# Loading each expert weight piece as two half transfers, each with a semaphore of its own, in a one-core hybrid diffusion step

## The chip, the cores and the metric

The kernel runs on one core of a Trainium2 chip. The metric is device time in microseconds (us) of one execution; lower is better. The time before is 1954.64 us, the median of three runs.

## The reference

One inference step of a hybrid backbone layer, on 384 tokens (128 context tokens, 256 latent tokens) of width 1024, in float32. A layer is a mixer (differential attention plus a two-way state space scan) and then a feed-forward part in which each of 16 experts chooses its tokens. The change touches the second part only:

```python
def expert_choice_ffn(h, w_router, w_gate, w_up, w_down):
    cap = EC_FACTOR * ntok // N_EXPERTS
    aff = jax.nn.softmax((xf @ w_router).astype(jnp.float32), axis=-1)
    gates, idx = lax.top_k(aff.T, cap)
    xe = xf[idx]
    he = jax.nn.silu(jnp.einsum('ecd,edf->ecf', xe, w_gate)) * jnp.einsum('ecd,edf->ecf', xe, w_up)
    ye = jnp.einsum('ecf,efd->ecd', he, w_down) * gates[..., None].astype(xe.dtype)
    out = jnp.zeros_like(xf).at[idx.reshape(-1)].add(ye.reshape(-1, d).astype(xf.dtype))
```

An expert sees 16 context and 32 latent tokens. Its three weight matrices hold 3 x 1024 x 2048 floats, 24 MB; all 16 experts hold 402.7 MB, and every byte is read from HBM once.

## The kernel before

**Mixer, routing, gather.** The first half of the program computes the mixer and the routing. Its weights come in 40 transfers of 2 MB (line 797) into two slots. Then the tokens of all experts are gathered.

**Pieces.** The expert weights lie in HBM as `in_expert_chunks[e, c]`, 16 experts of 12 pieces, 192 in all. A piece is 128 rows (one per partition) of 4096 floats, so 16 KB a row and 2,097,152 bytes a piece. Pieces 0 to 7 of an expert are alternate blocks of the gate and the up matrix, pieces 8 to 11 are blocks of the down matrix. SBUF (the program's name for its memory there is `arena`) has six slots of one piece each, and piece c goes to slot (c + 2) mod 6.

**TensorE (PE).** The loop of lines 731 to 786 runs over four groups of four experts. For each piece it waits once, at line 750, for `ff_slot{s}`, the semaphore that the piece's transfer raises by 16, and then issues 16 matmuls at line 765: eight steps k over 128 rows of the contraction, and in each two matmuls q that write the two halves of a PSUM bank. Step k reads floats 512k to 512k + 511 of each row of the slot. The last matmul of a piece raises one of three kinds of semaphore (`ff_used`, `gu_ready`, `d_ready0` or `d_ready1`). Between pieces stand small transposes of the hidden values (line 742). After four experts the outputs are combined (lines 784 and 786), and the next group starts.

**SyncE (SP).** SP issues all expert transfers, in order, at line 800 (`load`). The first six are issued while the mixer still ends. From piece 6 on, `wait_used` (lines 802 to 809) first waits for the semaphore by which PE tells that the piece six before, which lies in the same slot, has been used. The loop over experts is written with `sp.Fori`.

**Others.** ScalarE (ACT) and VectorE (DVE) work on the hidden values between the pieces; at line 1680 DVE writes the gathered tokens of one expert to `xe`.

Of the kernel before, what the change touches and what calls it, by code (L numbers as in the profile page):

```python
# [27 lines left out]
KT = D // P  # L28
EPS = 1e-6
CW = 512  # L30
# [13 lines left out]
FF_SLOTS = 6  # L44
# [20 lines left out]
EC = 12  # L65
# [67 lines left out]
def build(nc, t_in, t_out, consts, scratch):  # L133
    ctx = ExitStack()
    with ctx:
# [4 lines left out]
        def sem(name):  # L140
            if name not in sems:
                sems[name] = ctx.enter_context(nc.semaphore(name))
            return sems[name]
# [14 lines left out]
        slots = [at(16 * s, KT, CW) for s in range(FF_SLOTS)]  # L158
# [102 lines left out]
        mixer_w, expert_w, dt_cols = t_in["mixer_chunks"], t_in["expert_chunks"], t_in["dt_columns"]  # L261
# [21 lines left out]
        def _(pe):  # L283
# [128 lines left out]
            for ts in ((0,), (1, 2)):  # L412
                b = p_bank()
                for i, t in enumerate(ts):
                    for k in range(KT):
                        mm = pe.matmul(b[:, i * 64:(i + 1) * 64], h1T[:, k, t * P:(t + 1) * P], dt_w[:, k, :],
                                       start=k == 0, stop=k == KT - 1)
# [18 lines left out]
            for t in range(NT):  # L436
                pe.matmul(b[:, t * 64:t * 64 + 32], tri_f, tmp_a[:, t, 0:32], start=True, stop=True)
                mm = pe.matmul(b[:, t * 64 + 32:t * 64 + 64], tri_b, tmp_a[:, t, 32:64], start=True, stop=True)
            x_done(mm)
            b = x_bank()  # L440
            mm = pe.matmul(b[:, 0:NT * 64], ones, tmp_a[:, :, :], start=True, stop=True)
            x_done(mm)
            for d, tri in ((0, tri_f), (1, tri_b)):
                b = x_bank()
                for t in range(NT):
                    mm = pe.matmul(b[0:32, t * P:(t + 1) * P], tmp_a[:, t, 32 * d:32 * d + 32], tri,
                                   start=True, stop=True)
# [31 lines left out]
            for u, (g, t) in enumerate(units):  # L479
                if t == 0:  # L480
# [3 lines left out]
                    for d in range(2):  # L484
# [4 lines left out]
                mm = pe.matmul(b[:, 0:P], BC[:, g, TOK[t]:TOK[t] + P], BC[:, 4 + g, TOK[t]:TOK[t] + P],  # L489
                               start=True, stop=True)  # L490
# [3 lines left out]
                if t == 0:  # L494
                    for d in range(2):
# [3 lines left out]
                        for c in range(4):  # L499
                            mm = pe.matmul(b[:, c * P:(c + 1) * P], xdec[:, d, c * P:(c + 1) * P],  # L500
                                           BTM[:, 0, g * P:(g + 1) * P], start=True, stop=True)
                        x_done(mm)
                        AT.setdefault("st", []).append(n_x[0])
                if t == 1:
                    for d in range(2):
                        pe.wait_ge(sem("xdec_ready"), 4 * g + 2 + d + 1)
                        b = x_bank()
                        mm = pe.matmul(b[:, :], BTM[:, 1 + d, g * P:(g + 1) * P], xdec[:, d, :],
                                       start=True, stop=True)
# [10 lines left out]
                for h in range(S_HPG):  # L520
                    o = b[:, h * S_HD:(h + 1) * S_HD]
                    xh = xTM[:, t, h * S_HD:(h + 1) * S_HD]
                    mm = pe.matmul(o, ebuf[:, (2 * u) % 4, h, :], xh, start=True, stop=True)  # L523
                x_done(mm)
                if t:
                    if t == 1:
                        pe.wait_ge(sem("x_free"), hT1_at)
                    for d in range(2):
                        fresh = (t == 1) == (d == 0)
                        b = x_bank()  # L530
                        mm = pe.matmul(b[:, :], BC[:, 4 + g, TOK[t]:TOK[t] + P],  # L531
                                       h0T[:, d, :] if fresh else hT1[:, d, :], start=True, stop=True)
# [6 lines left out]
            for j in range(2):  # L539
                n0 = n_p[0]  # L540
                p_bank(4)
                for k2 in range(2):
                    w = chunk()
                    for ct in range(4):
                        for k in range(KT):
                            mm = pe.matmul(psum[:, (n0 + ct) % 4, 0:NTOK], w[:, k, ct * P:(ct + 1) * P],  # L546
                                           oT[:, k2 * KT + k, :], start=k2 == 0 and k == 0,
                                           stop=k2 == 1 and k == KT - 1)
# [64 lines left out]
            for i in range(NA + 5):  # L613
# [18 lines left out]
                if 3 <= i <= NA + 2:  # L632
# [4 lines left out]
                    for c, vb in kb:  # L637
                        mm = pe.matmul(b[:, 0:P], aT[:, (i - 3) % 2, c * P:(c + 1) * P],
                                       vT[:, vb, h * P:(h + 1) * P], start=c == 0, stop=c == len(kb) - 1)
# [61 lines left out]
            for n in range(4):  # L701
                pe.wait_ge(sem("diag2_ready"), 4 * (n + 1))
                b = p_bank()
                for q in range(4):
                    mm = pe.matmul(b[:, q * P:(q + 1) * P], ones, diag[:, n % 2, q, :], start=True, stop=True)
# [25 lines left out]
            with pe.Fori(0, NE // GE) as g:  # L731
                for i in range(GE):
                    pe.wait_ge(sem("xe_ready"), g * GE + (i + 1))

                    def h_to_cm(j):

                        pe.wait_ge(sem("h_done"), g * 16 + (4 * i + j + 3))
                        pe.wait_ge(sem("hT_done"), g * 16 + (4 * i + j + 1))
                        if i == 0 and j == 0:
                            pe.wait_ge(sem("comb_done"), g * 6 + 2)  # L740
                        for a in range(2):
                            mm = pe.transpose(psum[:, 4, a * P:(a + 1) * P], h_sb[:, j % 2, a * P:(a + 1) * P], ident)  # L742
                        mm.then_inc(sem("hT_psum"), 1)

                    for c in range(12):
                        s = (c + 2) % FF_SLOTS
                        if c == 8:
                            h_to_cm(3)
                            pe.wait_ge(sem("hT_done"), g * 16 + (4 * i + 5))
                        pe.wait_ge(sem(f"ff_slot{s}"), g * 128 + (32 * i + 16 * (c // 6 + 1)))  # L750
                        w = slots[s]
                        if c < 8:
                            j, up = c // 2, c % 2
                            bank, src, k0 = 2 * up + j % 2, xe, 0
                            if not up:
                                pe.wait_ge(sem("h_done"), g * 16 + (4 * i + j + 1))
                        else:
                            j, up = (c - 8) // 2, c % 2
                            bank, src, k0 = 5 + j, hT, KT * up
                            if not up:  # L760
                                pe.wait_ge(sem(f"d_free{j}"), g * GE + (i + 1))
                        first, last = c < 8 or not up, c < 8 or up
                        for k in range(KT):
                            for q in range(2):
                                mm = pe.matmul(psum[HALF * q:HALF * (q + 1), bank, 0:2 * P], src[:, k0 + k, :],  # L765
                                               w[:, k, 2 * P * q:2 * P * (q + 1)], start=bool(first and k == 0),
                                               stop=bool(last and k == KT - 1), tile_position=(0, HALF * q))
                        if c < 8:
                            mm.then_inc(sem("gu_ready" if up else "ff_used"), 1)
                            if up and j:  # L770
                                h_to_cm(j - 1)
                        else:
                            mm.then_inc(sem(f"d_ready{j}" if up else "ff_used"), 1)

                pe.wait_ge(sem("Gcur_ready"), g + 1)
                for j in range(2):
                    pe.wait_ge(sem(f"d_free{j}"), g * GE + (GE + 1))
                pe.wait_ge(sem("hT_done"), g * 16 + 17)
                for n, (t, half) in enumerate([(t, half) for t in range(NT) for half in range(2)]):
                    pe.wait_ge(sem("comb_done"), g * 6 + (n + 1))  # L780
                    bank = (7, 4)[n % 2]
                    cols_ = slice(half * CW, (half + 1) * CW)
                    if t:
                        mm = pe.matmul(psum[:, bank, :], Gs_cur[:, (t - 1) * P:t * P], stage_s[:, cols_], start=True, stop=True)  # L784
                    else:
                        mm = pe.matmul(psum[:, bank, :], Gp_cur, stage_p[:, cols_], start=True, stop=True)  # L786
                    mm.then_inc(sem("comb_ready"), 1)


        @block.sync  # L790
        def _(sp):
            sp.dma_start(cst, consts).then_inc(sem("const_in"), 16)
            for n in range(NM):
                if n >= 2:
                    name, value = AT["chunk_end"][n - 2]
                    sp.wait_ge(sem(name), value)
                sp.dma_start(slots[n % 2].rearrange("p k n -> p (k n)"), mixer_w[n]).then_inc(sem(f"w_in_slot{n % 2}"), 16)
            def load(e, c):
                s = (c + 2) % FF_SLOTS
                sp.dma_start(slots[s].rearrange("p k n -> p (k n)"), expert_w[e, c]).then_inc(sem(f"ff_slot{s}"), 16)  # L800

            def wait_used(e, c):

                if c >= 8 and c % 2:
                    sp.wait_ge(sem(f"d_ready{(c - 8) // 2}"), e + 1)
                elif c % 2:
                    sp.wait_ge(sem("gu_ready"), e * 4 + (c // 2 + 1))
                else:
                    sp.wait_ge(sem("ff_used"), e * 6 + (c // 2 + 1))

            for c in range(12):
                if c == 0:
                    sp.wait_ge(sem("ssd_over"), 1)
                if c == 2:
                    sp.wait_ge(sem("attn_over"), 1)
                if c == 4:
                    sp.wait_ge(sem("p_ready"), AT["chunk_end"][NM - 1][1])
                if c >= 6:
                    wait_used(0, c - 6)
                load(0, c)  # L820
            with sp.Fori(1, NE) as e:
                for c in range(12):
                    wait_used(e - 1 if c < 6 else e, (c - 6) % 12)
                    load(e, c)


        n_store = [0]
# [902 lines left out]
```

## Time and profile before

| | us |
|---|---|
| median of three runs (1953.71, 1954.64, 4177.42) | 1954.64 |
| the profiled execution: its own time | 1952.62 |
| its span, first to last instruction | 1950.8 |
| PE busy in the span, share | 1605.8, 82% |
| DVE busy | 526.8 |
| ACT busy | 256.9 |
| chain that ended last: share of expert transfers (in_expert_chunks) | 31% |
| chain that ended last: share of the expert matmuls (L765) | 14% |

Busy time is the union of an engine's instructions. The chain is followed back from the last instruction, at each step to what released it. The expert part takes the second half of the span, from about 992 us on. One transfer is cut by the hardware into packets, one for each row of the destination, which 16 DMA engines share; the profile tells packets of 4 bytes as well, by which a transfer raises its semaphore, one per engine.

### The profile page before, as it was taken

What the parts mean: (1) busy time and instruction counts of PE and PEld (TensorE: products, weight loads), DVE (VectorE), ACT (ScalarE), POOL (GpSimd) and SP (SyncE); (2) the same over time, 40 slices, a digit from 0 to 9 for tenths busy, and PEclk for the clock granted to TensorE, in tenths of its full rate; (3) what the DMA queues carried; (4) which work ended last, traced back from release to release, by engine and by line L of the source; (5) the groups of instructions that cost most, each with busy time, mean ns of one, the idle gap of its engine ahead of it and who ended that gap; (6) DMA issues with size and microseconds to landing.
All of it is one profiled execution on the core that took longest, in us unless ns stands there. A gap on an engine that the chain in (4) does not pass through costs nothing.

```text
span 1950.8 us, 22828 instructions
## 1 busy us (share of the span) xinstructions
PE 1605.8 (82%) x9379; PEld 950.4 (49%) x9379; DVE 526.8 (27%) x1455; ACT 256.9 (13%) x608; POOL 97.3 (5%) x126
## 2 busy tenths in 40 slices
PE   3997987998999977899698777887769777797775
PEld 1555445555566443454455444544436444364442
DVE  1338778771012034533520001100010000100002
ACT  1232222210010112201200001000010000100001
POOL 1002122120000000000000000000000000000000
PEclk9998999898999988799699999999999999999998
DMA  7124233222233212545259999999999999999993
GB/s 282 76 97 174 87 108 132 106 96 77 86 112 118 105 44 94 213 158 217 87 214 427 428 427 427 426 428 427 427 426 422 426 427 428 422 419 427 427 427 165
DMA packets 40924, 512.94 MB, mean 263 GB/s; under 512 B 4809, under 2 KB 5034, under 8 KB 11130
## 3 DMA queue, kind: packets, MB, share of 16 engines
q1 hardware_dynamic: 33552, 487.15, 60.2%
q0 software_dynamic: 6544, 22.66, 3.5%
q8 instruction: 79, 1.29, 0.3%
q10 hardware_dynamic: 730, 1.68, 0.2%
q14 instruction: 19, 0.16, 0.0%
HBM read 506.65 MB, written 4.82 MB: 262 GB/s over the span
## 4 chain that ended last, share of the span: by engine, by line
PE 52%; DMA 33%; DVE 9%; issue 2%; ACT 1%; POOL 1%; ACTq 0%; SPq 0%; DVEq 0%
DMA arena<-in_expert_chunks 31%; PE psum L333 16%; PE psum L765 14%; PE psum L344 8%; PE psum L546 4%; PE psum L357 1%; PE psum L382 1%; DMA arena<-in_w_subln 1%; PE psum L523 1%; DVE arena L1412 1%; PE psum L784 1%; DVE arena L1489 1%; PE psum L531 1%; DVE arena L1401 1%; PE psum L606 1%
## 5 line engine op out<-in xcount | busy, mean ns | idle before, releaser
L765 PE MATMUL psum<-arena 128*64 128x256 f32 x6144 | 707.5, 386 | 165.9 <-DMA arena<-in_expert_chunks 135.8
L765 PEld LDWEIGHTS psum<-arena 128*64 128x64 f32 x6144 | 433.2, 138 | 430.8 <-DMA arena<-in_expert_chunks 189.5
L333 PE MATMUL psum<-arena 128*128 128x384 f32 x1024 | 355.4, 507 | 10.7 <-ACT arena L1098 7.7
L333 PEld LDWEIGHTS psum<-arena 128*128 128x128 f32 x1024 | 202.3, 199 | 149.3 <-issue 22.3
L1688 DVE TENSOR_TENSOR arena<-arena,psum 128x256 f32<-128x256 f32 x64 | 26.9, 421 | 774.1 <-ACT arena L1153 774.1
L344 PE MATMUL psum<-arena 128*128 128x512 f32 x384 | 166.4, 592 | 1.8 <-DVE arena L1537 1.8
L344 PEld LDWEIGHTS psum<-arena 128*128 128x128 f32 x384 | 72.3, 190 | 90.2 <-issue 87.5
L1153 ACT ACTIVATE arena<-psum 128x256 f32<-128x256 f32 x64 | 24.6, 384 | 612.9 <-PE psum L765 612.9
L382 PE MATMUL psum<-arena 128*128 128x128 f32 (+1 forms) x301 | 57.7, 310 | 54.8 <-DMA arena<-in_g_post_ffn 17.0
L843 POOL TENSOR_TENSOR arena<-arena 128x1 f32<-128x1 f32 x48 | 28.1, 587 | 1224.1 <-DVE arena L1562 941.4
L546 PE MATMUL psum<-arena 128*128 128x384 f32 x256 | 86.0, 500 | 1.8 <-DVE arena L1370 1.2
L1160 ACT ACTIVATE arena<-psum 32x256 f32<-32x256 f32 x128 | 48.0, 375 | 275.2 <-PE psum L765 274.1
L382 PEld LDWEIGHTS psum<-arena 128*128 128x128 f32 (+1 forms) x301 | 39.1, 158 | 81.6 <-issue 45.6
L546 PEld LDWEIGHTS psum<-arena 128*128 128x128 f32 x256 | 49.9, 196 | 37.7 <-issue 2.7
L1412 DVE SCALAR_TENSOR_TENSOR arena<-arena 128x128 f32<-128x128 f32 x192 | 51.4, 344 | 0.0
L357 PE MATMUL psum<-arena 128*32 128x512 f32 x192 | 30.4, 786 | 12.6 <-ACT arena L1098 6.6
L742 PE MATMUL psum<-arena 128*128 128x128 f32 x128 | 27.6, 297 | 15.9 <-DVE arena L1675 15.9
L1098 ACT ACTIVATE arena<-psum,arena 128x384 f32<-128x384 f32 (+1 forms) x48 | 24.0, 505 | 125.0 <-DVE arena L1490 125.0
L523 PE MATMUL psum<-arena 128*128 128x64 f32 x192 | 28.7, 314 | 14.1 <-POOL arena L887 14.1
L606 PE MATMUL psum<-arena 64*128 64x384 f32 (+1 forms) x96 | 20.8, 518 | 23.2 <-ACT arena L1098 22.3
L1696 DVE TENSOR_TENSOR arena<-arena,psum 128x512 f32<-128x512 f32 x24 | 16.5, 687 | 86.0 <-PE psum L786 81.7
L1401 DVE TENSOR_SCALAR arena<-arena 128x128 f32<-128x128 f32 x192 | 38.6, 280 | 0.0
(238 smaller groups left out, 1001.4 us busy)
## 6 DMA issues: line engine op xcount, KB each, us to landing
arena<-in_expert_chunks SPq DMA_DIRECT2D x192, 2048.0 KB, 25.5
arena<-in_mixer_chunks SPq DMA_DIRECT2D x40, 2048.0 KB, 7.9
arena<-cs_rows POOLq DMA_DIRECT2D x24, 512.0 KB, 5.3
arena<-in_state_ssd POOLq DMA_DIRECT2D x8, 256.0 KB, 3.4
out_state<-arena POOLq DMA_DIRECT2D x8, 256.0 KB, 3.4
arena<-in_x_sample ACTq DMA_DIRECT2D x1, 1024.0 KB, 19.5
arena<-in_x_sample POOLq DMA_DIRECT2D x1, 1024.0 KB, 6.7
out_xs<-arena POOLq DMA_DIRECT2D x2, 512.0 KB, 2.9
```

What stands on the lines that cost most here:

```text
L333: mm = pe.matmul(b[:, 0:NTOK], w[:, k, ct * P:(ct + 1) * P], src[:, k, :], start=k == 0, stop=k == KT - 1)
L344: mm = pe.matmul(b[:, :], src[:, k, t * P:(t + 1) * P], w[:, k, :], start=k == 0, stop=k == KT - 1)
L357: mm = pe.matmul(b[32 * q:32 * q + 32, :], cond[:, k, :], w[:, k, :], start=k < 4, stop=k >= 4, tile_position=(0, 32 * q))
L382: mm = pe.transpose(b[0:width, at_:at_ + rows], src, ident[0:rows, 0:rows])
L523: mm = pe.matmul(o, ebuf[:, (2 * u) % 4, h, :], xh, start=True, stop=True)
L546: mm = pe.matmul(psum[:, (n0 + ct) % 4, 0:NTOK], w[:, k, ct * P:(ct + 1) * P], oT[:, k2 * KT + k, :], start=k2 == 0 and k == 0, stop=k2 == ...
L606: mm = pe.matmul(psum[:, (n + m) % 4, 0:kn], qT[r, h, t * P:(t + 1) * P], kT[r, h, k0:k0 + kn], start=True, stop=True)
L765: mm = pe.matmul(psum[HALF * q:HALF * (q + 1), bank, 0:2 * P], src[:, k0 + k, :], w[:, k, 2 * P * q:2 * P * (q + 1)], start=bool(first and ...
L843: pool.tensor_tensor(out, src, stat[:, 40:41], ALU.pow).then_inc(sem("pow_done"), 1)
L1160: cp = act.activation(dst[CAP_S * i:CAP_S * (i + 1), c0:c0 + 2 * P], psum[HALF * q + lo:HALF * q + lo + CAP_S, 5 + j, 0:2 * P], ACT.Copy)
L1401: last = dve.tensor_scalar(e_, e_, cs[:, t, 32 * d + 8 * g + h:32 * d + 8 * g + h + 1], 0.0, ALU.subtract, ALU.min)
L1412: last = dve.scalar_tensor_tensor(e_, e_, dt[:, t, 32 * d + 8 * g + h:32 * d + 8 * g + h + 1], cbm[:, u % 2, d, :], ALU.mult, ALU.mult)
```

## The change

Each piece is loaded by two transfers of 1 MB. Half 0 holds floats 0 to 2047 of every row (steps k = 0 to 3), half 1 the rest; both go to the same slot as before. A row of a transfer is now 8 KB. Each half has a semaphore of its own, `ff_slot{s}_0` and `ff_slot{s}_1`. PE waits for the first before its k = 0 and for the second before its k = 4, and its last matmul of k = 3 raises a new semaphore, `ff_half`. SP waits for `ff_half` before it loads half 0 of a slot again, and for the old semaphores before it loads half 1.

```diff
@@ PE
-                        pe.wait_ge(sem(f"ff_slot{s}"), g * 128 + (32 * i + 16 * (c // 6 + 1)))
...
                         for k in range(KT):
+                            if k % (KT // 2) == 0:
+                                pe.wait_ge(sem(f"ff_slot{s}_{2 * k // KT}"), g * 128 + (32 * i + 16 * (c // 6 + 1)))
                             for q in range(2):
...
+                            if k == KT // 2 - 1:
+                                mm.then_inc(sem("ff_half"), 1)
@@ SP
-            def load(e, c):
-                s = (c + 2) % FF_SLOTS
-                sp.dma_start(slots[s].rearrange("p k n -> p (k n)"), expert_w[e, c]).then_inc(sem(f"ff_slot{s}"), 16)
-
-            def wait_used(e, c):
-
-                if c >= 8 and c % 2:
+            def load(e, c, half):
+                s, n = (c + 2) % FF_SLOTS, KT // 2
+                sp.dma_start(slots[s][:, half * n:(half + 1) * n, :].rearrange("p k n -> p (k n)"),
+                             expert_w[e, c][:, half * n * CW:(half + 1) * n * CW]).then_inc(sem(f"ff_slot{s}_{half}"), 16)
+
+            def wait_used(e, c, half):
+
+                if not half:
+                    sp.wait_ge(sem("ff_half"), e * EC + (c + 1))
+                elif c >= 8 and c % 2:
...
-                if c >= 6:
-                    wait_used(0, c - 6)
-                load(0, c)
+                for half in range(2):
+                    if c >= 6:
+                        wait_used(0, c - 6, half)
+                    load(0, c, half)
             with sp.Fori(1, NE) as e:
                 for c in range(12):
-                    wait_used(e - 1 if c < 6 else e, (c - 6) % 12)
-                    load(e, c)
+                    for half in range(2):
+                        wait_used(e - 1 if c < 6 else e, (c - 6) % EC, half)
+                        load(e, c, half)
```

On SP, in the loop over experts, these rows stood for the first two pieces before. An ISA or REGISTER_ALU row works out the value that is waited for.

```order
L800 ISA [waits ff_used]
L800 DMA arena<-in_expert_chunks 128x4096
L807 ISA
L800 ISA [waits gu_ready]
L800 DMA arena<-in_expert_chunks 128x4096
```

And these stand for the same two pieces now.

```order
L803 ISA [waits ff_half]
L803 DMA arena<-in_expert_chunks 128x2048
L815 ISA
L803 ISA [waits ff_used]
L803 DMA arena<-in_expert_chunks 128x2048
L809 REGISTER_ALU
L803 ISA [waits ff_half]
L803 DMA arena<-in_expert_chunks 128x2048
L813 ISA
L803 ISA [waits gu_ready]
L803 DMA arena<-in_expert_chunks 128x2048
```

SP issues four DMAs of half the columns where it issued two, and has a wait before each; the order of the bytes is the same.

On PE, at the start of a group, the first two pieces were these rows before.

```order
L750 ISA [waits xe_ready]
L756 ISA [waits ff_slot2]
L765 MATMUL psum<-arena 64x256 [waits h_done]
L765 MATMUL psum<-arena 64x256 x15
L765 MATMUL psum<-arena 64x256 [waits ff_slot3]
L765 MATMUL psum<-arena 64x256 x15
```

And these now.

```order
L755 ISA [waits xe_ready]
L764 ISA [waits h_done]
L766 MATMUL psum<-arena 64x256 [waits ff_slot2_0]
L766 MATMUL psum<-arena 64x256 x7
L766 MATMUL psum<-arena 64x256 [waits ff_slot2_1]
L766 MATMUL psum<-arena 64x256 x7
L766 MATMUL psum<-arena 64x256 [waits ff_slot3_0]
L766 MATMUL psum<-arena 64x256 x7
L766 MATMUL psum<-arena 64x256 [waits ff_slot3_1]
L766 MATMUL psum<-arena 64x256 x7
```

The matmuls are the same 16 a piece in the same order; the second wait stands on the ninth of them.

## Rows read from the trace of the kernel before

**Rows 1.** The page, 40 equal slices of the span.

```profile
DMA  7124233222233212545259999999999999999993
GB/s 282 76 97 174 87 108 132 106 96 77 86 112 118 105 44 94 213 158 217 87 214 427 428 427 427 426 428 427 427 426 422 426 427 428 422 419 427 427 427 165
```

**Rows 2.** PE's waits, 992 to 1922 us: total us, times, longest us.

```profile
PE psum L765 <- DMA arena<-in_expert_chunks: 135.8, 119, 2.8
...
PE psum L765 <- DVE arena L1680: 3.2, 1, 3.2
```

**Rows 3.** The chain, 1040 to 1152 us: start us, us, what.

```profile
1060.82 0.04 issue
...
1064.71 25.46 DMA arena<-in_expert_chunks
1090.18 0.04 issue
...
1119.54 0.04 issue
...
1150.46 0.04 issue
```

**Rows 4.** SP's instructions of line 800: ns min/median/max, first and last start.

```profile
L800 SPq DMA_DIRECT2D arena<-in_expert_chunks x192: 327/333/433, 883.1 to 1896.2; - x192
L800 SPq FUSED_REGOPS  x180: 37/37/43, 1019.9 to 1896.1; - x180
...
DMA to landing us min/median/max: 7.6/25.5/27.1
```

**Rows 5.** DMA by queue, 1111 to 1120 us: packets, MB, share of 16 engines.

```profile
DMA packets 267, 3.85 MB, mean 428 GB/s; under 512 B 32, under 2 KB 32, under 8 KB 32
...
q1 hardware_dynamic: 267, 3.85, 100.5%
```

**Rows 6.** DMA by queue, 843.25 to 844.25 us, rows of 4 KB.

```profile
DMA packets 103, 0.40 MB, mean 401 GB/s; under 512 B 5, under 2 KB 5, under 8 KB 103
...
q0 software_dynamic: 103, 0.40, 97.6%
```

**Rows 7.** DMA by queue, 1058.6 to 1058.7 us, one instruction packet of 8 KB.

```profile
q14 instruction: 1, 0.01, 19.3%
```

**Rows 8.** DMA by queue, 1921.16 to 1921.18 us, one packet of 4 bytes.

```profile
q1 hardware_dynamic: 1, 0.00, 2.8%
```

**Rows 9.** L765's windows: us, PE busy (x instructions), granted clock, DMA share, GB/s.

```profile
992.74:994.00 1.26, 1.26 (x8) 0.63 0.00 0
994.00:995.00 1.00, 1.00 (x7) 0.50 0.00 0
...
1226.27:1228.00 1.73, 1.73 (x8) 0.50 1.02 436
```

**Rows 10.** SP in the timeline, its first issues after the first six.

```profile
998.13 10.69 SPq L800 DMA_DIRECT2D arena<-in_expert_chunks  x4
```

**Rows 11.** The chain between two groups of experts.

```profile
1209.26 3.67 PE psum L765 x32
1212.93 1.77 issue
...
1226.27 16.84 PE psum L765 x128
```

**Rows 12.** The chain at the end.

```profile
1896.21 25.41 DMA arena<-in_expert_chunks
1921.62 0.04 issue
1921.67 3.67 PE psum L765 x32
1925.34 1.77 issue
```

## The prediction

> **What bounds the kernel now.** I read the slices of the page first. From the slice at 990 us to the end the DMA digit is 9 and the rate stands at 419 to 428 GB/s [rows 1]: the expert part moves its 402.7 MB at one constant rate. Next the waits of PE: it waits 119 times for an expert transfer, 135.8 us in all [rows 2], so PE is the faster of the two, and the DMA engines set the pace. Then the chain, for the pace itself: six pieces land in 1090.18 - 1060.82 = 29.36 us, and again from 1090.18 to 1119.54 [rows 3], 4.893 us a piece of 2,097,152 bytes (428 GB/s). The third six take 30.92 us; seven such steps of about 1.5 us, in which instruction packets share the DMA engines, belong to the part, and I keep them as they are. PE needs 3.67 us for a piece [rows 12]. A transfer takes 25.5 us from issue to landing at the median and 7.6 at the least [rows 4]: about five are queued, and the fixed part, 7.6 - 4.9 = 2.7 us, is covered while they are.
>
> So the part has three terms: when the queue first starts, 186 pieces (7 to 192) at one pace, and what PE does after the last landing. Earlier release of slots, which half transfers give everywhere, counts at the first of them alone, since between them the DMA engines never run dry.
>
> **The start.** Pieces 1 to 6 are issued from 883.1 us on [rows 4], and PE's first wait at the expert matmuls is for DVE, not for a transfer [rows 2]; whatever these six cost more is covered by the routing. Piece 7 is issued at 998.13 [rows 10], when the first piece has been used. A piece's 16 matmuls show as 32 records in the trace, its half as 16. PE starts that piece at 992.74, after a wait, at a granted clock of 0.63 and then 0.50 (half speed, 1.2 GHz), and 8 + 7 records lie before 995.0 [rows 9], so that half 0 is used at about 995.1. It can then be issued 3.0 us earlier. It streams for 2.45 us and half 1 is still issued at 998.13, so the queue has a gap of half a microsecond and the gain is one half transfer, **-2.45 us**.
>
> **The end.** The last byte lands as late as the pace says. Then PE had 32 records, 3.67 us [rows 12]; now 16 of them have been done while half 1 was on its way (1.84 us of work against 2.45 us between landings), so **-1.84 us**. Combine and residual follow unchanged.
>
> **The pace.** The number of bytes is the same, that of the packets doubles: a piece was 8 packets of 16 KB on each of the 16 DMA engines and one of 4 bytes, and is now 16 of 8 KB and two of 4 bytes. What a packet costs beside its bytes decides. Three sizes can be read. The 4-byte packet takes 2.8% of 16 x 20 ns = 9 ns [rows 8]. 4 KB: 97.6% of 16 us is 15.62 us for 98 such packets and 5 of 4 bytes, 158.9 ns each [rows 6]. 16 KB: (4893 - 9) / 8 = 610.5 ns by the pace; the shares say 100.5% of 144 us less 32 x 9 ns, over 235 packets, 614.6 ns [rows 5], so successive packets overlap by some 4 ns. A line through 158.9 and 610.5 gives 36.75 ns for 1000 bytes and a fixed **8.4 ns** a packet, nearly all that the 4-byte packet takes, and for 8 KB 309.4 ns. The one 8 KB packet of the part, of another queue, took 19.3% of 1600 ns = 309 ns [rows 7]. A piece then takes 16 x 309.4 + 2 x 9 = 4968 ns, **75 ns more**, and 186 pieces 14.0 us; less 0.04 for the half piece already counted that is **+13.9 us**. In rate it is 428 to 422 GB/s.
>
> Bounds of this cost: if the overlap hides the fixed time wholly, 0; with the 614.6 ns of [rows 5] in the line the fixed part is 7 ns, a piece 65 ns, in all 12 us. From above: in [rows 6] the engines were idle 2.4% of the time; if that idleness is of the packets too, 4 KB cost 163.3 ns, the fixed part is 14 ns, a piece costs 123 ns more, in all 22.9 us. I take 75 ns, since two separate rows (the line and the single 8 KB packet) give the same.
>
> The Trainium skill (DMA: Bandwidth & Descriptors, "Why small descriptors are slow (HBM only)") states a fixed overhead of about 3 cycles a packet, beside one cycle for each 32 bytes. By it a 16 KB packet is 515 cycles and two of 8 KB are 518, 0.58% or 28 ns a piece, an estimate from the page; the sum below would then be +1.0 us. The rows speak for over twice that.
>
> **Waits and issues.** PE has one more wait a piece; where a landing releases it, the matmul starts 0.04 us later [rows 12], and PE has 4.89 - 3.67 = 1.2 us of slack a piece as cover. On PE no instruction is added for `ff_half`. SP issues twice as many transfers, 333 ns each plus 37 ns for the wait's value [rows 4]; 0.8 us of every 4.97. Behind the waiting SP only its own later transfers are queued, and half 0's wait ends before half 1's in any case. If this cover went, the first to be late would be the queue, which holds about five pieces.
>
> **Sum.** -2.45 - 1.84 + 13.9 = **+9.6 us**, against the profiled execution of 1952.62 us (span 1950.8): 1962.2. The median of the runs is 2.0 us above that execution, so I give 1954.64 + 9.6 = **1964**.
>
> **Rivals.**
>
> A, the packet's fixed time is hidden. The engine may start a packet while the one before still ends; the shares just over 100% [rows 5] speak for a little of it, the pace of 610.5 ns, which has no room below the line, against all of it. With none of the cost left the two gains stand alone: -4.3 us, 1950; with half of it 1957. The Trainium skill's figure above would land at 1956.
>
> B, the queue takes a number of transfers, not of bytes. Between groups PE stops: its last piece ends at 1212.93 and the next group starts at 1226.27 [rows 11], its first 16 records taking until about 1229.2 at half clock (8 in the first 1.73 us, [rows 9]). Before, five or six pieces of 4.89 us bridged this. If only six transfers can be under way, six halves last 6 x 2.48 = 14.9 us, to 1227.8; the next is issued at 1229.2 and moves bytes 2.7 us later, so 4.1 us are lost at each of three pauses: +9.6 + 12.3, 1976. Nothing in the trace shows such a limit, since six slots never allowed more.
>
> C, on the slow side: transfers of 1 MB with 8 KB rows stream no better than the only small-row stretch of the trace, 401 GB/s over all its time [rows 6], because the engines idle between the packets of successive transfers. That is 2,097,152 / 401 = 5.230 us a piece, 0.337 more: 62.7 - 4.3 = +58 us, 2013. It decides, that is it passes 2% or 39 us, from 0.233 us a piece on, a pace of 5.13 us. Against it: on the queue of SP the pace before is its packets' time and nothing else. The Trainium skill (DMA: Bandwidth & Descriptors, "Rules for kernel authors") asks for at least 1 MiB a transfer for bandwidth; these are at that size, and no run here yet shows one smaller or equal on this queue.
>
> **How the numbers follow.** The forecast 1964 (1959 to 1969 with its roundings and scatter between runs) has 0.66. A has 0.20, B 0.05, C 0.04, and 0.05 is left for what I don't see. The range starts at A's end, 1950, since main case and B alone hold too little, and goes to the upper bound of the packet cost, 1954.6 + 22.9 - 4.3 = 1973; it leaves out C and most of B. A measurement of this kernel can tell some 2% (39 us) from no change. Only C and part of the unseen lie above, nothing that I know of lies 2% below: faster 0.01, same 0.94, slower 0.05.
>
> **What would show it.** In the slices of the expert part 421 or 422 GB/s at a full DMA digit; twelve landings of halves in 29.8 us in the chain instead of six in 29.36; SP's first issue after the first twelve at about 995.1; 16 records of PE after the last landing instead of 32. PE's waits for transfers become shorter and about twice as many. I am wrong if the rate stays at 427 (A), if there are slices well under 420 at the three pauses (B), or if the pace is above 5.1 us (C).

## The result, and the profile after

The changed kernel takes 1966.11 us, the median of five runs (1963.93 to 1969.04). The ratio to the kernel before is 1.0061, 95% interval 1.0045 to 1.0076: slower by 0.6%, which is within the 2% that the chances speak of. One of the five executions of the kernel before took 4177.42 us, and the ratio leaves it out. The profiled execution took 1966.84 us, its span is 1965.0, against 1952.62 and 1950.8 before.

The page, 40 slices, answers to [rows 1]:

```profile
DMA  7224233222233213535269999999999999999993
GB/s 283 78 107 157 87 107 124 112 96 76 86 121 115 96 43 125 195 141 215 86 257 421 421 421 420 421 421 421 421 421 420 421 421 421 421 420 421 421 420 163
```

The DMA digit is 9 as before, and the rate under it is 420 to 421 GB/s, where it was 419 to 428 and mostly 426 to 428. The engines are as busy and move less.

The chain of waits of the changed kernel in the stream, which answers to [rows 3]:

```profile
1050.05 23.45 DMA arena<-in_expert_chunks
1073.49 0.04 issue
...
1079.90 25.93 DMA arena<-in_expert_chunks
1105.83 0.14 issue
...
1108.08 4.00 SPq L803
...
1112.32 1.93 SPq L803
```

Thirteen halves land between 1073.49 and 1105.83: 32.34 / 6.5 = 4.975 us a piece, 82 ns more than the 4.893 of before, where 75 was forecast. There is something new in the chain: an issue of SP takes 1.9 or 4.0 us, where the prediction had 0.33. The line of SP's issues, answering to [rows 4], has it as well:

```profile
L803 SPq DMA_DIRECT2D arena<-in_expert_chunks x384: 327/1897/5248, 886.5 to 1910.0; - x192
...
DMA to landing us min/median/max: 5.1/26.5/29.0
```

PE's waits, answering to [rows 2], became twice as many and shorter, as was forecast:

```profile
PE psum L766 <- DMA arena<-in_expert_chunks: 124.0, 240, 1.8
```

The start and the end of the stream, in the chain, which answer to [rows 12] and to the first of the windows of [rows 9]:

```profile
996.06 15.72 PE psum L766 x128
...
1909.99 27.55 DMA arena<-in_expert_chunks
1937.54 0.04 issue
1937.58 1.95 PE psum L766 x16
1939.53 1.77 issue
```

Two things are to be read. PE is done 1.99 us after the last landing (1939.53 - 1937.54) instead of 3.72. And its first expert matmul starts at 996.06 instead of 992.74, though nothing before it was changed. From PE's start to the last landing is 941.48 us, before it was 1921.62 - 992.74 = 928.88: the stream itself is 12.6 us longer. With the 1.7 us at the end and the 3.3 of the mixer part, 12.6 - 1.7 + 3.3 = 14.2, the whole difference of the spans.

### The profile page after: what moved, and what is told of

It is laid out like the page before. It is cut to its first block, busy times and chain, and to the rows that moved or that the text cites. A ratio compares the mean times of both kernels' runs of the same rounds, so it can differ in the third digit from the quotient of the medians.

```text
span 1965.0 us, 23548 instructions
## 1 busy us (share of the span) xinstructions
PE 1632.1 (83%) x9379; PEld 947.1 (48%) x9379; DVE 526.6 (27%) x1455; ACT 256.7 (13%) x608; POOL 97.3 (5%) x126
## 4 chain that ended last, share of the span: by engine, by line
PE 49%; DMA 32%; DVE 9%; SPq 5%; issue 3%; ACT 1%; POOL 1%; ACTq 0%; DVEq 0%
DMA arena<-in_expert_chunks 30%; PE psum L333 16%; PE psum L766 10%; PE psum L344 8%; SPq L803 4%; PE psum L546 4%; PE psum L357 1%; PE psum L382 1%; DMA arena<-in_w_subln 1%; DVE arena L1420 1%; PE psum L523 1%; PE psum L787 1%; DVE arena L1497 1%; PE psum L531 1%; DVE arena L1409 1%
## 5 line engine op out<-in xcount | busy, mean ns | idle before, releaser
L766 PE MATMUL psum<-arena 128*64 128x256 f32 x6144 | 731.9, 387 | 152.5 <-DMA arena<-in_expert_chunks 124.0
L766 PEld LDWEIGHTS psum<-arena 128*64 128x64 f32 x6144 | 428.4, 138 | 446.5 <-DMA arena<-in_expert_chunks 199.4
## 6 DMA issues: line engine op xcount, KB each, us to landing
arena<-in_expert_chunks SPq DMA_DIRECT2D x384, 1024.0 KB, 26.5
```

## The experiments

All were timed beside the kernel before on the same chip. The median of before there was 1953.72 us for the first four, 1954.16 for the next four and 1953.43 for the last two. "Stream" is the time from PE's first expert matmul to the last landing, read from each trace as above; "pace" is the time of one piece, from landings in the chain.

| kernel | us | ratio, 95% interval | packets | transfers a piece | pace us | stream us |
|---|---|---|---|---|---|---|
| before | 1954.64 | | 16 KB | 1 | 4.893 | 928.9 |
| changed | 1966.11 | 1.0061 (1.0045 to 1.0076) | 8 KB | 2 | 4.975 | 941.5 |
| e1_whole_gates | 1968.27 | 1.0078 (1.0065 to 1.0091) | 8 KB | 2 | 4.97 | 942.5 |
| e2_rows64 | 2810.41 | | 16 KB | 2 | | |
| e7_alternate_rows | 1954.05 | 0.9998 (0.999 to 1.0007) | 16 KB | 2 | 4.895 | 928.8 |
| e8_one_transfer_8k | 1967.97 | 1.0073 (1.006 to 1.0086) | 8 KB | 1 | 4.97 | 942.4 |
| e3_quarters | 1994.86 | 1.0212 (1.0199 to 1.0225) | 4 KB | 4 | 5.108 | 971.0 |
| e5_pairs_32k | 1967.94 | 1.0065 (1.0047 to 1.0084) | 32 KB | 1/2 | 4.853 | 939.4 |
| e4_ends_only | 1952.89 | 0.9999 (0.999 to 1.0007) | 16 KB, 8 pieces of 8 KB | 1, 2 | | 928.0 |
| e6_pairs_cut_ends | 1950.62 | 0.9985 (0.9977 to 0.9994) | mostly 32 KB | mixed | | 925.1 |
| e9_pairs_small_ends | 1946.58 | 0.9964 (0.995 to 0.9977) | mostly 32 KB | mixed | | 924.3 |
| e10_changed_again | 1966.30 | 1.0065 (1.0051 to 1.0078) | 8 KB | 2 | | 942.0 |

### Packet or transfer

The change doubles both the packets and the transfers. Three kernels take them apart.

**e1_whole_gates** keeps the loads in halves and takes the early release and the early use away:

```diff
-                            if k % (KT // 2) == 0:
-                                pe.wait_ge(sem(f"ff_slot{s}_{2 * k // KT}"), g * 128 + (32 * i + 16 * (c // 6 + 1)))
+                            if k == 0:
+                                for half in range(2):
+                                    pe.wait_ge(sem(f"ff_slot{s}_{half}"), g * 128 + (32 * i + 16 * (c // 6 + 1)))
...
-                if not half:
-                    sp.wait_ge(sem("ff_half"), e * EC + (c + 1))
-                elif c >= 8 and c % 2:
+                if half:
+                    return
+                if c >= 8 and c % 2:
```

> Two transfers of 1 MB a piece with rows of 8 KB, as in the changed kernel, but with the waits of the kernel before: SP issues both halves when the whole piece in the slot is used, and PE waits for both before a piece. Nothing is left out. My theory: the pace is the changed kernel's, 4.97 us a piece, and both gains are gone: about 1.9 us later at the start (half 0 is issued with half 1) and 1.7 us later at the end (32 records of PE after the last landing instead of 16), so 1966.1 + 3.6 = 1970 us. Rival, early release gave nothing: 1966 us, as the changed kernel.

1968.27 us. Set against the changed kernel by their ratios to before, 1.0078 and 1.0061, it is some 3 us slower, with intervals that overlap (2.5 us against e10, 1.0065). Its trace has PE done 1940.13 - 1936.33 = 3.80 us after the last landing, 1.8 more than the changed kernel, as expected, but the stream is only 1.0 us longer (0.5 against e10's), not 1.9. The loads in halves alone cost 13.6 us of stream.

**e2_rows64** and **e7_alternate_rows** make two transfers of 64 rows of 16 KB each, so the packets are those of before; both keep e1's waits.

```diff
# e2, against e1
-                sp.dma_start(slots[s][:, half * n:(half + 1) * n, :].rearrange("p k n -> p (k n)"),
-                             expert_w[e, c][:, half * n * CW:(half + 1) * n * CW]).then_inc(sem(f"ff_slot{s}_{half}"), 16)
+                sp.dma_start(slots[s][HALF * half:HALF * (half + 1)].rearrange("p k n -> p (k n)"),
+                             expert_w[e, c][HALF * half:HALF * (half + 1), :]).then_inc(sem(f"ff_slot{s}_{half}"), 16)
# e7, against e1, in place of the same lines
+                sp.dma_start(slots[s][half::2].rearrange("p k n -> p (k n)"),
+                             expert_w[e, c][half::2, :]).then_inc(sem(f"ff_slot{s}_{half}"), 16)
```

> Two transfers of 1 MB a piece, split by partitions: 64 rows of 16 KB each, with the waits of the kernel before. As many transfers as in the changed kernel, but the packets are of 16 KB again. If the loss is a fixed time of each packet: only the second 4-byte packet is left, 4.893 + 0.009 = 4.902 us a piece and 1954.6 + 1.7 = 1956 us. If the loss is one of each transfer: 4.97 us a piece, 1970 us. It also tells what makes SP's issues take 1.9 us at the median in the changed kernel: if the queue holds a number of transfers (about 11), they do so here as well; if it holds a number of packets (about 11 x 128), 12 transfers of 64 packets fit in it and an issue takes 0.33 us.

2810.41 us, 44% above before (single executions 2711.74 to 2819.94, so no ratio is given, but the shortest is 39% above). It answers another question than was asked. The queue over 100 us of the stream (1500 to 1600 us) of e2:

```profile
DMA packets 1686, 22.15 MB, mean 222 GB/s; under 512 B 334, under 2 KB 334, under 8 KB 334
...
q1 hardware_dynamic: 1683, 22.10, 100.7%
```

The 16 engines are busy all the time and move half as much: a packet of 16 KB takes (1.007 x 1600 us) / 1349 = 1.19 us instead of 0.61. So transfers of 64 neighbouring rows run at half rate here, and the miss was in the design; e7 puts it right by giving each half every other row. Since e7 takes every other row in HBM as well as in SBUF, the two don't tell which of the two sides made e2 slow.

> Two transfers of 1 MB a piece as in e2_rows64, but half 0 takes the even partitions and half 1 the odd ones, 64 rows of 16 KB each, with the waits of the kernel before. In e2 a 16 KB packet took twice its time; if that came from 64 neighbouring partitions, it is gone here. Loss per packet: 4.902 us a piece, 1953.7 + 1.7 = 1955.5 us. Loss per transfer: 4.97 us a piece, 1968 us. If 64 rows are slow wherever they lie: about 2800 us.

1954.05 us, ratio 0.9998. The same view of e7:

```profile
DMA packets 3256, 42.73 MB, mean 427 GB/s; under 512 B 648, under 2 KB 648, under 8 KB 648
...
q1 hardware_dynamic: 3251, 42.65, 100.4%
```

427 GB/s with twice the transfers and semaphores of before. Of the 9 ns of a second 4-byte packet at most 2 show in the pace (six pieces in 1091.30 - 1061.93 = 29.37 us, before 29.36). Splitting a piece in two transfers costs nothing that can be measured, if the packets stay whole.

**e8_one_transfer_8k** is the counterpart: one transfer and one semaphore a piece, but HBM holds the piece as two blocks, so that no packet can be longer than 8 KB.

```diff
-    expert = np.empty((NE, EC, P, KT * CW), np.float32)
+    expert = np.empty((NE, EC, 2, P, KT * CW // 2), np.float32)
...
-            expert[e, c] = by_partition(block)
+            expert[e, c] = by_partition(block).reshape(P, 2, -1).transpose(1, 0, 2)
...
-                sp.dma_start(slots[s].rearrange("p k n -> p (k n)"), expert_w[e, c]).then_inc(sem(f"ff_slot{s}"), 16)
+                sp.dma_start(slots[s].rearrange("p (h k) n -> p h (k n)", h=2), expert_w[e, c].rearrange("h p n -> p h n")).then_inc(sem(f"ff_slot{s}"), 16)
```

> The kernel before, with one transfer of 2 MB and one semaphore a piece and its waits, but each piece lies in HBM as two blocks of 128 rows x 8 KB, so that every packet is of 8 KB. If the loss is a fixed time of each packet: 16 x 309.5 + 9 = 4.961 us a piece, 68 ns more, 12.7 us: 1953.7 + 12.7 = 1966 us. If it is one of each transfer or semaphore: 4.893 us a piece, 1954 us.

1967.97 us. The queue of e8 from 1500 to 1600 us:

```profile
DMA packets 5454, 42.11 MB, mean 421 GB/s; under 512 B 320, under 2 KB 320, under 8 KB 320
...
q1 hardware_dynamic: 5448, 42.01, 100.9%
```

With the kernel of before in all but the length of a packet (and the layout in HBM that makes it), the loss is there in full: 421 GB/s, a stream of 942.4 us. This and e7 settle the cause. It is the packets.

### The price of a packet at other sizes

**e3_quarters** and **e5_pairs_32k** are written with a list of transfers for each expert, in quarters of a piece (first quarter, number of quarters). SP issues the list and PE waits at the first quarter of each transfer:

```diff
+def items(i):
+    return [(u, 1) for u in range(4 * EC)]           # e3
+    return [(u, 8) for u in range(0, 4 * EC, 8)]     # e5
...
+                            if k % 2 == 0 and 4 * c + k // 2 in ends(i)[0]:
+                                name, m = ends(i)[0][4 * c + k // 2]
+                                pe.wait_ge(sem(name), g * (16 * ends(i)[1][name]) + 16 * m)
```

For pairs HBM holds pieces c and c + 1 side by side for each partition.

> Four transfers of 512 KB a piece, rows of 4 KB, each with a semaphore of its own; PE waits for a quarter before its two steps, SP issues quarters 0 and 1 after the first half of a piece is used and 2 and 3 after all of it. By the fixed time of a packet: 32 x 158.9 + 4 x 9 = 5121 ns a piece, 228 more than before, 42.4 us over 186 pieces; start -1.9, end -2.8 (one quarter left after the last landing): 1954.6 + 37.7 = 1992 us, if the queue doesn't run dry. If it holds only 11 transfers (or 1400 packets, the same here), it holds 11 x 1.28 = 14.1 us of work; the pause between groups is 13.3 us and the first half piece after it 3.0, the fixed part of a transfer 2.7, so 4.9 us are lost at each of three pauses: 2007 us.

1994.86 us, 2.9 above the first number. The chain of e3:

```profile
1072.15 0.04 issue
...
1092.58 0.04 issue
```

Sixteen quarters, four pieces, in 20.43 us, 5.108 us a piece (5.121 expected). And its windows of the pauses between the first and the second and between the second and the third group:

```profile
1210.00:1250.00 40.00, 31.12 (x214) 16.15 (x212) 5.34 (x11) 5.05 (x11) 0.00 (x0) 0.91 1.03 408
1450.00:1490.00 40.00, 30.24 (x196) 15.09 (x198) 4.72 (x9) 4.28 (x9) 0.00 (x0) 0.91 1.03 408
```

408 GB/s in these two pauses as in the rest (last column): the queue didn't run dry, and the 2007 us of the second number were wrong. The third pause (1700 to 1740 us) has 401; the kernel before has 411 there too, against 426 in its first. The ratio's interval, 1.0199 to 1.0225, holds 1.02.

> The law of the packet tried upward: two neighbouring pieces (c and c + 1, which lie side by side in SBUF) are laid side by side in HBM too and loaded by one transfer of 4 MB with rows of 32 KB; SP waits for the second piece of a pair to be used. With a fixed 8.6 ns a packet a pair takes 8 x (8.6 + 2 x 602) + 9 = 9.71 us instead of 9.787, 7.2 us less over 93 pairs. Against it: the first refill is issued 3.5 us later, the last landing leaves two pieces (3.7 us), and three pair slots don't bridge the pause between groups: 21.7 us of work is left when PE stops, the next issue comes 23.4 us later and needs 2.7 more, 4.4 us lost at each of three pauses, 13 us. Sum +13: 1967 us. If rows over 16 KB are cut into packets of 16 KB the pace doesn't change: 1974 us.

1967.94 us, 0.9 above the sum. The chain gives 1094.14 - 1065.02 = 29.12 us for three pairs, 4.853 us a piece, 40 ns less than before, so rows of 32 KB are not cut. The losses that were expected against it are there too. Its windows of the first pause, and of the end in the chain:

```profile
1220.00:1260.00 40.00, 32.39 (x240) 18.84 (x242) 6.67 (x14) 3.48 (x7) 0.00 (x0) 0.91 0.90 377
```

```profile
1933.08 0.14 issue
1933.22 7.13 PE psum L785 x64
```

377 GB/s over 40 us against 432 in the stream is 5.1 us lost (4.4 expected), and 7.3 us of PE follow the last landing. The second and third pause have 344 GB/s (1460 to 1500 us) and 376 (1700 to 1740).

The packet's fixed time from each pair of paces: 32 KB to 16 KB, 4 packets more and half a 4-byte packet, (40 - 4.5) / 4 = 8.9 ns; 16 to 8 KB with one transfer (e8: 29.80 us for six pieces from 1062.06 to 1091.86, 4.967) 74 / 8 = 9.2 ns; 16 to 4 KB (215 - 27) / 24 = 7.8 ns. These take 9 ns for a 4-byte packet; with the 2 ns at most that e7 leaves for it the first and the last are 9.8 and 8.7 ns. It is one price of 8 to 10 ns over a factor of eight in size.

### Where the small grain pays

**e4_ends_only** loads only piece 6 of the first and piece 11 of the fourth expert of each group in halves.

> Whole pieces of 2 MB as before, except piece 6 of the first expert and piece 11 of the last expert of each group of four, which are loaded in halves: 8 of 192 pieces. Cost 8 x 0.078 = 0.6 us; the gain at the start (1.9) and at the end (1.7) stays: 1954.6 - 3.0 = 1951.6 us, and 4.893 us a piece for the rest. Rival: without the halves in between the early release and the early use give nothing, 1955 us.

1952.89 us, 0.9999 (0.999 to 1.0007). Its stream is 0.9 us shorter and its PE is done 2.3 us after the last landing (1922.12 to 1924.46), 1.4 sooner than before. The signs are as expected and the sum of 2.3 us is below what the timing can tell; the run is inconclusive on time.

**e6_pairs_cut_ends** and **e9_pairs_small_ends** put the long packets in the middle and small transfers where they are waited for:

```diff
     out = [(u, 8) for u in range(0, 4 * EC, 8)]
     if i == 0:
-        out[3:4] = [(24, 2), (26, 2), (28, 4)]                             # e6
+        out[3:5] = [(24, 2), (26, 2), (28, 4), (32, 4), (36, 4)]           # e9
     if i == GE - 1:
-        out[5:6] = [(40, 4), (44, 2), (46, 2)]                             # e6
+        out[4:6] = [(32, 4), (36, 4), (40, 4), (44, 2), (46, 2)]           # e9
```

> As the pairs of 32 KB rows, but the first refill in each group is cut in two halves and a single piece, and the last pair of each group in a single piece and two halves, so that the pauses, the start and the end have the small grain. 85 pairs save 77 ns each (6.5 us), 8 pieces in halves cost 0.6; start -1.5, end -1.8; no time lost at pauses (the first half is issued 16.3 us after the stop, against 21.7 us of queued work): 1953.7 - 9.2 = 1944.5 us. If rows over 16 KB are cut by the hardware: 1951 us. If the pauses run dry all the same: up to 13 us more.

1950.62 us, faster than before (0.9977 to 0.9994) but 6 us short of the sum. The expectation of e9, which follows, names what its trace shows of that: waits of the queue right after the start, and 4.4 us of PE after the last landing where 1.9 were expected. How the rest divides was not found out.

> As e6_pairs_cut_ends, with single pieces 8 and 9 after the first refill of each group and before its last pieces as well. In e6's trace the queue was dry for 2.2 and 1.1 us right after the start, since a pair can be issued only when both of its pieces are used, and PE had 4.4 us of work left after the last landing, since a pair lands as one lump. Cutting both should give back 3.3 and 2.0 us, and costs 8 more pairs made single, 0.6 us: e6's 1950.6 - 4.7 = 1946 us. Rival, those waits were made up for later in the stream: 1951 us.

1946.58 us, ratio 0.9964 (0.995 to 0.9977): the fastest of all, 7 us or 0.36% below before and some 20 us below the change, and within 1 us of the 1946 expected. In its stream three pairs land in 1099.04 - 1069.89 = 29.15 us. Its profiled execution, at 1951.13 us, was the slowest of its five, and in it the gain at the end did not come: PE carried 5.7 us of work past the last landing, where 2.4 were expected. PE's timeline shows a part of the reason (start, us, what, and the idle time before it):

```profile
1888.97 7.13 PE L790 MATMUL psum<-arena 128*64 128x256 f32 x64 [2.20 <-DMA arena<-in_expert_chunks]
1896.03 0.44 PE L765 MATMUL psum<-arena 128*128 128x128 f32 x2
1898.62 8.81 PE L790 MATMUL psum<-arena 128*64 128x256 f32 x64 [2.15 <-DMA arena<-in_expert_chunks]
```

PE had waited 2.15 us for a pair, and the granted clock of the next 2 us was 0.52 (from 1898.6 to 1900.6), so two pieces took 8.81 us instead of 7.13. That is 1.7 of the 3.3 us; what made the rest is open. A wait as long doesn't always cost clock: the one of 2.20 us before it was followed by a clock of 1.00 and by 7.13 us. By this trace (stream 4.6 us shorter than before, end 2.0 us longer) the gain is 2.6 us; the other four executions, at 1946.1 to 1946.8, have no trace, so where their further 4 us came from was not seen.

**e10_changed_again** is the changed kernel once more.

> The changed kernel as it is, on this chip, for its time beside the other versions and for the start of the expert part in its trace. 1966 us. The mixer part, which the change doesn't touch, ran 3.3 us later in the changed kernel's trace (first expert matmul at 996.1 instead of 992.7); in the experiments it began at 993.2 to 994.4. If that was chance, it begins there here too.

1966.30 us. Its first expert matmul starts at 992.74, as before the change, the last landing is at 1934.77 and PE is done at 1936.77. So the 3.3 us of the mixer part in the first trace were chance between executions and none of the change; this execution's span is 1962.3, 11.5 us over that of before, and its time 1964.06.

## Why the prediction was right

**The sum.** +9.6 us was forecast and +11.5 measured (1954.64 to 1966.11); e10 gives +12.9 against its own runs of before, 1953.43. The range held it, the sign was right, and the rival that would have hidden the cost (A) is excluded: by e8 the packets cost 13.5 us of stream. The terms, from the traces, are +13.6, -1.7 and, for the start, -0.5 to -1.0.

**The pace** (+13.9 forecast). Right in mechanism and size. e1, which has the loads in halves and no gain, has a stream 942.5 - 928.9 = 13.6 us longer. The fixed time of 8.4 ns from packets of 4 and 16 KB came out as 8 to 10 in four kernels. A piece cost 74 ns more in e8, and 82 in the thirteen halves of the changed kernel. Those 82 are above the mean: over 186 pieces they would be 15.3 us, more than the 13.6. A part of this difference is in the steps with instruction packets, which the prediction kept as they are: they were 1.5 us each (six stand in the trace after 1040 us, where it counts seven in the part) and are 1.1 to 1.3 us in the changed kernel. The about 3 cycles of the Trainium skill (DMA: Bandwidth & Descriptors, "Why small descriptors are slow (HBM only)") would have made 28 ns a piece, an estimate; the 74 and 82 ns measured here decide against it. The second half of the term, 9 ns for another 4-byte packet, was too much: in e7 it shows as 2 at most. The price of a piece was put together as 8 x 8.4 + 9 and is rather 8 x 9.2.

**The end** (-1.84). Measured -1.73 (3.72 to 1.99 us after the last landing).

**The start** (-2.45). This is the term of the sum that was mis-sized: -2.45 us were forecast, and -0.5 to -1.0 came, which is most of the 1.9 us by which the sum was too low. First, "half 0 is used at about 995.1", 2.4 us after PE's start, was read from windows that count a record in both windows it touches, and by its start; SP's issue came 3.49 us after PE's start (999.55 - 996.06; e10 has 3.52), only 1.9 sooner than before (5.39). Second, what was issued sooner didn't arrive as much sooner: against e1, which issues both halves at 5.39, the stream of the changed kernel is 1.0 us shorter, that of e10 0.5, so the gain is hardly more than the 0.5 us by which these two traces of one kernel differ. The windows (GB/s in the last column) show where it goes, both from about 2.5 us after SP's first issue on. The changed kernel first, which issues at 999.55, and then e1, which issues at 999.2:

```profile
1002.00:1004.00 2.00, 2.00 (x22) 1.00 0.98 373
1004.00:1006.00 2.00, 2.00 (x23) 1.00 0.94 373
1006.00:1008.00 2.00, 2.00 (x22) 1.00 1.01 389
```

```profile
1002.00:1004.00 2.00, 2.00 (x22) 1.00 1.01 422
1004.00:1006.00 2.00, 2.00 (x22) 1.00 1.01 426
1006.00:1008.00 2.00, 2.00 (x22) 1.00 1.02 430
```

With halves issued one at a time, 1.7 to 1.9 us apart, the engines run for 6 us at 373 to 389 GB/s; with two halves issued together they are at once at 422 to 430. (426 - 378 GB/s) x 6 us is 0.29 MB or 0.7 us. That looks like a queue with too little in it, but the other traces don't settle it. e4 issues a first half and, 1.96 us later, a second, and is slow as well; e6 does the same with 1.88 us between them and isn't. Their windows, again from about 2.5 us after the first issue on (997.56 in e4, 997.38 in e6), 4 us each, e4 first:

```profile
999.60:1003.60 4.00, 4.00 (x40) 2.75 (x38) 0.20 (x1) 0.39 (x1) 0.00 (x0) 1.00 0.95 358
```

```profile
999.40:1003.40 4.00, 4.00 (x42) 2.72 (x39) 0.27 (x1) 0.38 (x1) 0.00 (x0) 1.00 1.02 420
```

The halves of e6 come from rows of 32 KB in HBM, those of e4 from rows of 16 KB. Whether that makes the difference was not tried, so why the early half lost most of its lead stays open.

**Rival B** was wrong twice over. There is a limit: with halves SP's issues take 1.9 us at the median, and from issue to landing pass 26.5 us, 10.7 transfers; with quarters 15.5 us, 12.1 transfers. By these it lies near 11 or 12 transfers of 128 packets; in e1, with some 10 under way, the median issue is 333 ns again. Whether it is one of transfers or of packets the runs don't tell, since e2 and e7, with 64 packets a transfer, have no more than 12 to issue (medians 468 and 475 ns). But it costs nothing that shows. The prediction's 0.8 us of SP for a piece were 3.8 (two issues of 1.9), and the rate stayed at 421 GB/s. By the same argument a lower limit wouldn't have cost either, though none was tried, since what SP can't put into the queue waits in front of it with its slot free, and is issued as the queue drains. What bridges a pause is the free slots, in bytes; e3's 408 GB/s in the pauses show it, and e5, which has few transfers but whole pairs as slots, runs dry. The mistake was to count the issue that was blocked by the queue as one blocked by PE.

**Rival C** (5.13 us a piece and more) is excluded for 8 KB; e3, with 4 KB, comes to 5.108, just under the 5.13 from which it was to decide; its ratio of 1.0212 has an interval that holds 2%.

## What to carry to other kernels

Where the DMA engines are busy all the time, time is bytes plus a fixed price for each packet, and a packet is a run that is contiguous on both sides (in e8 a cut in HBM alone was enough to shorten it). A finer grain should be bought with more transfers of whole rows (or only at the first and last pieces, where someone waits for it), not with shorter rows throughout; and longer rows can be had from the layout alone, as long as small transfers stay at the start, at pauses and at the end.

Before a gain from an earlier issue is added up, see what the resource behind it does with it: here the stream was at its limit at all times but two, so 186 early releases were worth 0.5 to 1 us (and the early use at the end 1.7), while the shorter rows that came with them cost 14.

## What the runs showed of the hardware that was not expected

- A transfer of 64 neighbouring rows into 64 neighbouring partitions uses all 16 DMA engines and runs at half rate (222 GB/s, 1.19 us for 16 KB); with every other row and partition it runs at the full 427 GB/s. Which of the two sides decides was not tried.
- Two transfers of 64 rows instead of one of 128 cost no time (ratio 0.9998), though each has its own semaphore and SP's issue takes 475 ns instead of 333.
- With some 11 transfers of 128 packets under way, a further issue holds SP longer (median 1.9 us with halves, 0.9 with quarters, 5.2 at the longest), without a loss of rate in the stream.
- After PE had waited 2.15 us for a transfer, its granted clock was 0.52 for the next 2 us; after a wait of 2.20 us, 10 us earlier in the same trace, it was 1.00. The kernels with pairs, where the waits are longer, have a mean granted clock of 0.95 from 1040 to 1900 us (e5, e6, e9), the kernel before 0.99.
